# Splitting three down slabs of each hosted feed-forward block, with its convolution taps dealt out anew

## Chip, cores and metric

The kernel runs on one core of a Trainium2 chip. The metric is the device time of one execution in microseconds. TensorE (PE) multiplies, VectorE (DVE), ScalarE (ACT) and GpSimd (POOL) compute elementwise, SyncE (SP) issues the loads.

## The reference

256 tokens and 256 context tokens of width 1024, all in fp32. Three kinds of layers follow one another: a hybrid mixer, a conformer convolution and a window attention, with four feed-forward blocks between them. Two parts matter here.

```python
def conv_ffn(h, w_up, w_dw, b_dw, w_down):          # width 2816, 3 taps
    u = dwconv(h @ w_up, w_dw, b_dw)
    a, b = jnp.split(u, 2, axis=-1)
    return (jax.nn.silu(a) * b) @ w_down
...
    v = a * jax.nn.sigmoid(g)                        # conformer, width 1024
    v = dwconv(v, w_dw, b_dw)                        # 31 taps
    v = jax.nn.silu(layernorm(v, ln_g, ln_b))
    return v @ w_pw2 + b_pw2
```

The first block's feed-forward (ffn0) doesn't depend on the convolution of the context, and that of the context (ffn_ctx) not on the convolution of the tokens, so each can run beside the other.

## The kernel before

Features lie on partitions, tokens along the free axis. All weights come as slabs of 1 MB (`raw`, 128 x 2048 fp32) in a ring of 3 slots, in one fixed order (`KEYS`). Most slabs are split: ScalarE writes the upper part `whi` (fp32r, `hi`), VectorE and GpSimd subtract it for the lower part `wlo` (`lo`, 1536 and 512 columns here), and TensorE makes three fp32r products, upper by upper, upper by lower, lower by upper (`mm3`). A slab in `kept_whole()` isn't split and is multiplied in plain fp32.

A feed-forward block walks 11 pairs j (`NJ`) of 256 hidden columns. Pair j has two up slabs (numbers 3j-1 and 3j) and one down slab (3j+4). TensorE's order is up(j), then down(j-1). An up product is 48 matmuls of 128x256 into bank 2*par or 2*par+1, par = j % 2. In ffn0 and ffn_ctx all down slabs are whole (`DOWN_WHOLE`), 16 fp32 matmuls each, two records apiece in the trace. In ffn_lat and ffn2 they are split, and the middle value too (`m_hi` by ScalarE, `m_lo` by VectorE).

Per pair ScalarE makes `whi` of the next pair's first up slab, the centre tap of half 0 (`tap`), `whi` of the second, the tap of half 1, and silu. VectorE makes its part of `wlo` and the other two taps of a half (`taps`, 4 operations that read PSUM) twice, and then the middle value cvb = silu(a) * b, which the down product reads.

Both blocks also host a 31-tap convolution: v is in `vpad` (in tile `gates`), the sum in `acc` (tile `sra`). Tap 0 with the bias is `dwconv_first`, 8 operations ahead of the block. 22 taps are products by ScalarE (`product`, 8 operations into bufA or bufB in turn) which VectorE adds (`add_product`, one 128x2048 operation); 8 are VectorE's own (`own_tap`, 8 multiply-adds on SBUF). `host(j, par, at)` is called at three places of a pair. Products 3 a pair for j = 2 to 7; an own tap in each of the pairs 0 to 7, after the second add. ScalarE's product n may start when product n-2 has been added. From pair 8 on the layer norm takes the places.

The engines run in order; semaphores bind them. SyncE's load into a slot waits, where the slab before it in the slot is whole, until TensorE has used it (`slab_done`); where it is split, until both lower parts are made (`lo_done`, `lo2_done`). The queue is in order, so the loads behind wait too.

## Time and profile before

| | us |
|---|---|
| median of 3 runs (1394.03 to 1399.96) | 1394.24 |
| the profiled execution, its own time | 1395.78 |
| its span | 1394.0 |
| TensorE busy | 1368.9 (98%) |
| VectorE busy | 963.2 (69%) |
| ScalarE busy | 824.4 (59%) |
| GpSimd busy | 464.9 (33%) |

The span runs from the first instruction to the last; the chain that ended last follows from the last instruction back to what released each. Busy shares are means over stages with different limits, so the two hosted blocks have to be looked at by themselves. Records of matmuls overlap, so one is longer than the step from one to the next; in the timelines of the other engines too neighbours overlap by about 0.08.

### The profile page before, as it was taken

What the parts mean: (1) busy time and instruction counts of PE and PEld (TensorE: products, weight loads), DVE (VectorE), ACT (ScalarE), POOL (GpSimd) and SP (SyncE); (2) the same over time, 40 slices, a digit from 0 to 9 for tenths busy, and PEclk for the clock granted to TensorE, in tenths of its full rate; (3) what the DMA queues carried; (4) which work ended last, traced back from release to release, by engine and by line L of the source; (5) the groups of instructions that cost most, each with busy time, mean ns of one, the idle gap of its engine ahead of it and who ended that gap; (6) DMA issues with size and microseconds to landing.
All of it is one profiled execution on the core that took longest, in us unless ns stands there. A gap on an engine that the chain in (4) does not pass through costs nothing.

```text
span 1394.0 us, 27113 instructions
## 1 busy us (share of the span) xinstructions
PE 1368.9 (98%) x10606; PEld 1270.8 (91%) x10606; DVE 963.2 (69%) x1298; ACT 824.4 (59%) x1190; POOL 464.9 (33%) x190
## 2 busy tenths in 40 slices
PE   7999999999999999999999999999999999999997
PEld 4878889999999999899999999999998868999996
DVE  3312674857899987769899979766667696654446
ACT  3542565645788837567888565555544486644554
POOL 1443434234232321242222201655552201233332
PEclk9999999999999999999999999999999999999999
DMA  8776775455344434774444447556554613455451
GB/s 310 257 272 240 260 281 186 156 218 184 122 181 181 168 153 193 258 279 160 158 160 166 180 189 254 223 213 213 213 185 185 261 47 132 181 181 181 181 184 58
DMA packets 39573, 272.04 MB, mean 195 GB/s; under 512 B 4612, under 2 KB 5892, under 8 KB 6974
## 3 DMA queue, kind: packets, MB, share of 16 engines
q1 hardware_dynamic: 39486, 270.81, 52.1%
q8 instruction: 63, 1.03, 0.3%
q14 instruction: 24, 0.20, 0.0%
HBM read 269.73 MB, written 1.06 MB: 194 GB/s over the span
## 4 chain that ended last, share of the span: by engine, by line
PE 92%; DVE 4%; ACT 2%; DMA 1%; issue 1%; SPq 0%; POOL 0%; DVEq 0%; ACTq 0%
PE ps L1985 23%; PE ps L1986 23%; PE ps L1987 23%; PE ps L655 10%; PE ps L2131 3%; PE ps L2022 2%; DMA raw<-w_dram 1%; PE ps L2032 1%; PE ps L2499 1%; PE ps L2485 1%; DVE wlo L1340 1%; ACT whi L845 1%; PE ps L2434 1%; PE ps L2181 1%; DVE tiny L1833 0%
## 5 line engine op out<-in xcount | busy, mean ns | idle before, releaser
L803 POOL TENSOR_TENSOR wlo<-raw,whi 128x1024 fp32r<-128x1024 f32 (+2 forms) x181 | 462.6, 2557 | 908.9 <-ACT whi L845 908.9
L845 ACT ACTIVATE whi<-raw 128x2048 fp32r<-128x2048 f32 x181 | 345.4, 1911 | 392.6 <-PE ps L1987 232.9
L1340 DVE TENSOR_TENSOR wlo<-raw,whi 128x1024 fp32r<-128x1024 f32 (+2 forms) x181 | 312.7, 1728 | 319.6 <-ACT whi L845 318.7
L1985 PE MATMUL ps<-h_hi,whi 128*128 128x256 f32 x1232 | 354.1, 287 | 0.0
L1986 PE MATMUL ps<-h_lo,whi 128*128 128x256 f32 x1232 | 348.5, 283 | 0.0
L1987 PE MATMUL ps<-h_hi,wlo 128*128 128x256 f32 x1232 | 348.4, 283 | 0.0
L1985 PE MATMUL ps<-g_hi,whi 128*128 128x256 f32 x1040 | 298.4, 287 | 0.0
L1986 PE MATMUL ps<-g_lo,whi 128*128 128x256 f32 x1040 | 294.2, 283 | 0.0
L1987 PE MATMUL ps<-g_hi,wlo 128*128 128x256 f32 x1040 | 294.1, 283 | 0.0
L1985 PEld LDWEIGHTS ps<-h_hi,whi 128*128 128x128 f32 x1232 | 236.0, 192 | 8.1 <-issue 6.8
L1986 PEld LDWEIGHTS ps<-h_lo,whi 128*128 128x128 f32 x1232 | 236.1, 192 | 0.8
L1987 PEld LDWEIGHTS ps<-h_hi,wlo 128*128 128x128 f32 x1232 | 236.1, 192 | 0.0
L1985 PEld LDWEIGHTS ps<-g_hi,whi 128*128 128x128 f32 x1040 | 199.4, 192 | 3.7 <-issue 2.9
L1986 PEld LDWEIGHTS ps<-g_lo,whi 128*128 128x128 f32 x1040 | 199.4, 192 | 0.4
L1987 PEld LDWEIGHTS ps<-g_hi,wlo 128*128 128x128 f32 x1040 | 199.4, 192 | 0.0
L655 PE MATMUL ps<-cvb,raw 128*128 128x256 f32 x704 | 155.3, 379 | 0.0
L655 PEld LDWEIGHTS ps<-cvb,raw 128*128 128x128 f32 x704 | 132.5, 190 | 17.4
L563 DVE SCALAR_TENSOR_TENSOR cvb<-ps,cols,cvb 128x255 f32<-128x255 f32 (+1 forms) x176 | 76.6, 476 | 11.3 <-ACT cvb L485 6.7
L563 DVE SCALAR_TENSOR_TENSOR cva<-ps,cols,cva 128x255 f32<-128x255 f32 (+1 forms) x176 | 76.6, 476 | 10.4 <-ACT cva L485 5.2
L942 ACT ACTIVATE bufB<-gates,cols 128x256 f32 (+1 forms) x176 | 72.7, 499 | 14.6 <-DVE sra L1462 14.6
L942 ACT ACTIVATE bufA<-gates,cols 128x256 f32 (+1 forms) x176 | 72.7, 499 | 13.0 <-DVE sra L1462 13.0
L1985 PE MATMUL ps<-m_hi,whi 128*128 128x256 f32 x208 | 58.9, 283 | 0.0
(317 smaller groups left out, 1858.4 us busy)
## 6 DMA issues: line engine op xcount, KB each, us to landing
raw<-w_dram SPq DMA_DIRECT2D x243, 1024.0 KB, 4.8
sra<-w_dram SPq DMA_DIRECT2D x2, 1024.0 KB, 5.8
mqk<-w_dram SPq DMA_DIRECT2D x2, 1024.0 KB, 6.7
brev<-w_dram SPq DMA_DIRECT2D x2, 1024.0 KB, 7.1
gates<-w_dram SPq DMA_DIRECT2D x2, 1024.0 KB, 8.5
xlat<-xT_dram SPq DMA_DIRECT2D x2, 512.0 KB, 4.6
brev<-w_first_keys_dram SPq DMA_DIRECT2D x1, 1024.0 KB, 9.0
brev<-bias_rows SPq DMA_DIRECT2D x1, 1024.0 KB, 8.5
```

The lines of the kernel that those rows point to most:

```text
L563: ins = dve.scalar_tensor_tensor(out, ps[:, 2 * par + half, m * T + src:m * T + src + n], w, out, ALU.mult, ALU.add)
L655: ins = pe.matmul(ps[:, 4 + m // 2, (m % 2) * T:(m % 2) * T + T], wf[:, k, m * P:m * P + P], cvb[:, par, k, :], start=(first and k == 0 an ...
L803: pool.tensor_tensor(wlo[:, g.slot, part], raw[:, g.slot, part], whi[:, g.slot, part].bitcast(F32), ALU.subtract).then_inc(lo2_done, 1)
L845: act.activation(whi[:, g.slot, :], raw[:, g.slot, :], ACT.Copy).then_inc(hi_done, 1)
L942: ins = act.activation(buf[:, t * T:t * T + T], vpad[:, t, bass.ds(k, T)], ACT.Copy, scale=w)
L1340: dve.tensor_tensor(wlo[:, g.slot, part], raw[:, g.slot, part], whi[:, g.slot, part].bitcast(F32), ALU.subtract)\
L1985: pe.matmul(out, w[0], x[0], start=start, stop=False, skip_group_check=True)
L1986: pe.matmul(out, w[0], x[1], start=False, stop=False, skip_group_check=True)
L1987: return pe.matmul(out, w[1], x[0], start=False, stop=stop, skip_group_check=True)
L2022: pe.matmul(ps[:, bank, m * T:m * T + T], w[i][:, k, m * P:m * P + P], x[0][:, k, :], start=(k == 0 and m == 0 and i == 0), stop=False, sk ...
L2032: ins = pe.matmul(ps[:, bank, m * T:m * T + T], w[:, k, m * P:m * P + P], x[1][:, k, :], start=False, stop=(k == KT - 1), skip_group_check ...
L2131: ins = pe.matmul(ps[r:r + QUAD, bank, 0:SLABC], cnd[:, c:c + QUAD], w[:, t, :], start=(t < 4 and k == 0), stop=(t >= 4 and k == n - 1), s ...
```

## The change

The down slabs of pairs 2, 4 and 6 of ffn0 and ffn_ctx are split (`DOWN_SPLIT`), with the middle value of these pairs, by new semaphores. The taps are dealt out anew: 25 products instead of 22 (three in each of the pairs 0 to 7 and one in pair 8), own taps only in pairs 1, 3, 5, 7, now between the second and the third product, and own tap 2 in front of the block (`early_tap`). `dwconv_first`, that tap and the first two products are made in pieces among the pw1 slabs. In pairs 0 to 7 silu and the middle value come ahead of the second product and its add. In a split pair ScalarE makes the down slab's `whi` and `m_hi`, and VectorE its `wlo` and `m_lo`, ahead of the third product. The pairs of hosted blocks are written out on ScalarE and VectorE instead of a loop.

```diff
-PRODUCTS = 22
+DOWN_SPLIT = (2, 4, 6)
+ADD_SLOTS = [(j, at) for j in range(NJ - 3) for at in range(3)] + [(NJ - 3, 0)]
+OWN_SLOTS = [j for j in range(1, NJ - 3) if j not in DOWN_SPLIT]
+PRODUCTS = len(ADD_SLOTS)
+OWN_TAPS = [2] + [4 * j for j in OWN_SLOTS]
+PRODUCT_TAPS = [k for k in range(1, CONV_TAPS) if k not in OWN_TAPS]
+assert len(PRODUCT_TAPS) == PRODUCTS
...
-            out.append(use != ffn or (i >= 4 and i % 3 == 1))
+            out.append(use != ffn or (i >= 4 and i % 3 == 1 and (i - 4) // 3 not in DOWN_SPLIT))
...
+                if whole and j - 2 in DOWN_SPLIT:
+                    act.wait_ge(hostmid_lo, host_mid(f, j - 2))
                 tap(1, j, par)
-                if host:
+                hosting = host and j < NJ - 3
+                if host and not hosting:
                     host(j, par, 1)
                 act.wait_ge(conv_out, 2 * j + (f * 2 * NJ + 1))
                 act.activation(cva[:, par, :, :], cva[:, par, :, :], ACT.Silu).then_inc(silu_done, 1)
-                if host:
+                if hosting:
+                    host(j, par, 1)
+                if host and not host_split(j, par):
                     host(j, par, 2)
 
             def split(j, par, first):
-                if whole:
+                if whole and not host_split(j, par):
                     return
                 act.wait_ge(mid_f, j + (f * NJ + 1))
+                if whole:
+                    act.wait_ge(slab_done, down_slab(b0, j - 2) + 1)
+                    act.activation(m_hi[:, par, :, :], cvb[:, par, :, :], ACT.Copy).then_inc(hostmid_hi, 2)
+                    host(j, par, 2)
+                    return
...
             if host:
-                with act.Fori(0, 3) as jj:
-                    for u in range(2):
-                        up(Slab(b0 + 5 + 3 * u, 2, jj), 2 * jj + (2 + u), u, False)
-                for j in (NJ - 3, NJ - 2):
-                    up(Slab(b0 + 3 * j - 1), j, j % 2, False)
+                for j in range(2, NJ - 1):
+                    g = Slab(b0 + 3 * j - 1)
+                    up(g, j, j % 2, False)
+                    hi(g + (2 + RING))
+                    split(j, j % 2, False)
...
                 taps(1, j, par)
-                if beside:
+                hosting = beside and j < NJ - 3
+                if beside and not hosting:
                     beside(1)
                 dve.wait_ge(silu_done, j + (f * NJ + 1))
                 dve.wait_ge(conv_out, 2 * j + (f * 2 * NJ + 2))
                 dve.tensor_tensor(cvb[:, par, :, :], cva[:, par, :, :], cvb[:, par, :, :], ALU.mult).then_inc(mid_f, 1)
-                if beside:
+                if hosting:
+                    beside(1)
+                if beside and not host_split(j, par):
                     beside(2)
                 if down:
                     lo(g + (2 + RING))
+                if whole and host_split(j, par):
+                    dve.wait_ge(hostmid_hi, host_mid(f, j))
+                    dve.tensor_tensor(m_lo[:, par, :, :], cvb[:, par, :, :], m_hi[:, par, :, :].bitcast(F32), ALU.subtract)\
+                       .then_inc(hostmid_lo, 2)
+                    beside(2)
...
             pair(Slab(b0 + 2), 1, 1, True, hosted(1, 1))
-            with dve.Fori(0, 3 if host else 4) as jj:
-                order.enter(jj, 8 + (2 * KT if host else 0))
-                for u in range(2):
-                    j = 2 * jj + (2 + u)
-                    pair(Slab(b0 + 5 + 3 * u, 2, jj), j, u, True, hosted(j, u))
-                order.leave(3 if host else 4)
             if host:
-                for j in (NJ - 3, NJ - 2):
+                for j in range(2, NJ - 1):
                     pair(Slab(b0 + 3 * j - 1), j, j % 2, True, hosted(j, j % 2))
...
-                if whole:
+                plain = whole and not host_split(j, par)
+                if plain:
                     pe.wait_ge(landed[g.slot], g.landings())
                     pe.wait_ge(mid_f, j + (f * NJ + 1))
                     wf = raw[:, g.slot, :].rearrange("p (k n) -> p k n", k=2)
                 else:
                     pe.wait_ge(lo_done, g.split() + 1)
                     pe.wait_ge(lo2_done, g.split() + 1)
-                    pe.wait_ge(mid_lo, j + (fs * NJ + 1))
+                    if whole:
+                        pe.wait_ge(hostmid_lo, host_mid(f, j))
+                    else:
+                        pe.wait_ge(mid_lo, j + (fs * NJ + 1))
...
-            def product(q, n, k, buf):
-
-                if not isinstance(n, int) or n >= 2:
+            def product(q, n, t0=0, t1=KT):
+
+                k, buf = PRODUCT_TAPS[n], (bufA, bufB)[n % 2]
+                if n >= 2:
                     act.wait_ge(prod_used, n + (PRODUCTS * q - 1))
-                for t in range(KT):
...
+                else:
+                    act.wait_ge(v_done, 4 * q + t1 // 2)
+                    act.wait_ge(pads_done, 2)
+                for t in range(t0, t1):
+                    ins = act.activation(buf[:, t * T:t * T + T], vpad[:, t, k:k + T], ACT.Copy, scale=col("dw_w", KT * k + t))
+                if t1 == KT:
+                    ins.then_inc(prod_done, 1)
...
                 def host(j, par, at):
-                    if not isinstance(j, int) or j < 2:
-                        early = isinstance(j, int)
-                        if at == 2 and early:
-                            return
-                        if early and j == 0 and at == 0:
-                            act.wait_ge(v_done, 4 * q + 4)
-                            act.wait_ge(pads_done, 2)
-                        n, k = (2 * j + at, 3 * j + (1 + at)) if early else (3 * j + (at - 2), 4 * j + (at - 1))
-                        product(q, n, k, (bufA, bufB)[at if early else (par + at) % 2])
-                    if isinstance(j, int) and (j, at) == (NJ - 2, 1):
+                    if (j, at) == (0, 0) and q == 0:
+                        product(q, 0, 6, KT)
+                        product(q, 1, 6, KT)
+                    if (j, at) in ADD_SLOTS[1:-1]:
+                        product(q, ADD_SLOTS.index((j, at)) + 1)
...
                 hi(Slab(b1 + 3 + RING))
                 glu(q, 2, b1 + 3)
                 hi(Slab(b1 + 4 + RING))
+                act.wait_ge(xlo_done, KT // 2 * n + KT // 2)
+                product(q, 0, 0, 6)
                 hi(Slab(b1 + 5 + RING))
                 glu(q, 3, b1 + 5)
+                product(q, 1, 0, 6)
...
             c = hi_to(c, "pw1_lat", 7)
+            product(1, 0, 0, 6)
             c = hi_to(c, "ffn_ctx", 0)
             c = hi_to(c, "ffn_ctx", 1)
             group_rows("ada_a")
             glu(1, 3, done("pw1_lat", 7) - 1)
             c = hi_to(c, "ffn_ctx", 2)
+            product(1, 0, 6, KT)
+            product(1, 1)
...
                 fold(n, sq)
                 lo(Slab(b1 + 1 + RING))
                 glu(q, 1)
+                dwconv_first(q, 2, 4)
                 scale(n, x, gains, y)
                 lo(Slab(b1 + 2 + RING))
                 split_lo(i, y, out, shift)
                 lo(Slab(b1 + 3 + RING))
                 glu(q, 2)
+                dwconv_first(q, 4, 6)
                 lo(Slab(b1 + 4 + RING))
+                early_tap(2, 6)
                 lo(Slab(b1 + 5 + RING))
                 glu(q, 3)
-
-            def dwconv_first(q):
-
-                dve.wait_ge(v_done, 4 * q + 4)
+                dwconv_first(q, 6, KT)
+                early_tap(6, KT)
...
+            def own_tap(k, t0=0, t1=KT):
+
+                for t in range(t0, t1):
+                    order.mark(dve.scalar_tensor_tensor(acc[:, t, :], vpad[:, t, k:k + T], col("dw_w", KT * k + t), acc[:, t, :],
+                                                        ALU.mult, ALU.add))
+
+            def early_tap(t0, t1):
+
+                dve.wait_ge(dve_order, order.value())
+                own_tap(OWN_TAPS[0], t0, t1)
...
-                    if isinstance(j, int) and j < 2:
-                        if (j, at) == (1, 0):
-                            add_product(q, 1, bufB)
-                        if at == 1:
-                            add_product(q, 2 * j, bufA)
-                            own_tap(q, 2 * j + 1, 3 * j + 3)
-                    elif not isinstance(j, int):
-                        n = 3 * j + (at - 3)
-                        add_product(q, n, bufs[(par + at + 1) % 2])
-                        if at == 1:
-                            own_tap(q, n + 1, 4 * j + 2)
-                    elif (j, at) == (NJ - 3, 0):
-                        add_product(q, PRODUCTS - 1, bufs[(PRODUCTS - 1) % 2])
+                    if at == 2 and j in OWN_SLOTS:
+                        dve.wait_ge(prod_used, ADD_SLOTS.index((j, 1)) + 1 + PRODUCTS * q)
+                        own_tap(OWN_TAPS[1 + OWN_SLOTS.index(j)])
+                    if (j, at) in ADD_SLOTS:
+                        n = ADD_SLOTS.index((j, at))
+                        add_product(q, n, bufs[n % 2])
                     elif (j, at) == (NJ - 3, 2):
...
                 x = flat(xlat[:, 2 * k:2 * k + 2, :])
                 dve.tensor_tensor(x, ps[:, 4 + k, :], x, ALU.add).then_inc(x_ready, 1)
+                if k == 0:
+                    dwconv_first(0, 0, 2)
+                if k == 1:
+                    early_tap(0, 2)
             pw1_dve(0, BASE["pw1_ctx_b"], 2, 2, xlat, bufB, lambda t: col("norm_ffn", t), bufA, G, None)
 
 
-            dwconv_first(0)
...
             c = lo_to(c, "pw1_lat", 6)
+            dve.wait_ge(xlo_done, KT // 2 * 5)
+            dwconv_first(1, 0, 4)
             glu(1, 2)
+            dwconv_first(1, 4, 6)
             c = lo_to(c, "pw1_lat", 7)
+            early_tap(0, 6)
             c = lo_to(c, "ffn_ctx", 0)
             c = lo_to(c, "ffn_ctx", 1)
             glu(1, 3)
+            dwconv_first(1, 6, KT)
             c = lo_to(c, "ffn_ctx", 2)
+            early_tap(6, KT)
             group_add("ada_a")
             modulated(4, 6, mod2_done, GROUPS.index("ada_a") + 1)
 
 
-            dwconv_first(1)
```

VectorE at the end of a pair, in the loop before (par 0): own tap, middle value, add, next lower half.

```order
L1469 ISA
L1469 SCALAR_TENSOR_TENSOR sra<-gates,cols,sra 128x256
L581 REGISTER_ALU
L583 TENSOR_TENSOR cvb<-cva,cvb 128x512
L1458 REGISTER_ALU
L1462 TENSOR_TENSOR sra<-sra,bufB 128x2048
L1339 REGISTER_ALU
L1340 TENSOR_TENSOR wlo<-raw,whi 128x1536
```

The same place after, in a pair with an own tap (3 of ffn0): the middle value stands ahead of add and own tap.

```order
L609 TENSOR_TENSOR cvb<-cva,cvb 128x512
L1510 TENSOR_TENSOR sra<-sra,bufA 128x2048
L1515 SCALAR_TENSOR_TENSOR sra<-gates,cols,sra 128x256 x8
L1510 TENSOR_TENSOR sra<-sra,bufB 128x2048
L1383 TENSOR_TENSOR wlo<-raw,whi 128x1536
```

And in the split pair 4: no own tap, the third lower half and m_lo ahead of the third add.

```order
L609 TENSOR_TENSOR cvb<-cva,cvb 128x512
L1510 TENSOR_TENSOR sra<-sra,bufB 128x2048
L1383 TENSOR_TENSOR wlo<-raw,whi 128x1536
L618 TENSOR_TENSOR m_lo<-cvb,m_hi 128x512
L1510 TENSOR_TENSOR sra<-sra,bufA 128x2048
L1383 TENSOR_TENSOR wlo<-raw,whi 128x1536
```

The add of the third product moved behind two operations that wait for the down slab. ScalarE at the end of a pair, in the loop before: the last of the second product, silu, the first operation of the third.

```order
L942 ISA
L942 ACTIVATE bufB<-gates,cols 128x256
L505 REGISTER_ALU
L506 ACTIVATE cva<-cva 128x512
L939 REGISTER_ALU
L942 ISA
L942 REGISTER_ALU
L942 ACTIVATE bufA<-gates,cols 128x256
```

ScalarE after, split pair 4 of ffn_ctx: silu is ahead of the second product, the down slab's whi and m_hi ahead of the third.

```order
L524 ACTIVATE cva<-cva 128x512
L982 ACTIVATE bufA<-gates,cols 128x256 x8
L882 ACTIVATE whi<-raw 128x2048
L536 ACTIVATE m_hi<-cvb 128x512
L982 ACTIVATE bufB<-gates,cols 128x256 x8
L882 ACTIVATE whi<-raw 128x2048
```

Silu moved one product forward; whi and m_hi stand where the third product began.

## Rows read from the trace of the kernel before

**Rows 1.** The page: the chain that ended last, share of the span by engine.
```profile
PE 92%; DVE 4%; ACT 2%; DMA 1%; issue 1%; SPq 0%; POOL 0%; DVEq 0%; ACTq 0%
```

**Rows 2.** Sums: ffn0, ffn_ctx; PE, PEld, DVE, ACT, POOL busy (count), clock, DMA share, GB/s.
```profile
339.30:543.20 203.90, 203.90 (x1416) 194.61 (x1416) 178.04 (x229) 151.47 (x274) 57.48 (x22) 1.00 0.41 160
624.60:829.00 204.40, 204.40 (x1419) 194.98 (x1419) 186.17 (x234) 151.55 (x274) 52.78 (x23) 1.00 0.42 165
```

**Rows 3.** The chain in order of time (start, us, what): whole down products.
```profile
380.74 6.91 PE ps L655 x32
399.15 6.91 PE ps L655 x32
...
776.93 7.11 PE ps L655 x32
```

**Rows 4.** Timeline of VectorE (start, us, operation, out<-in, count, idle before), ffn0's loop.
```profile
403.02 1.76 DVE L1340 TENSOR_TENSOR wlo<-raw,whi 128x1536 fp32r<-128x1536 f32 x1
...
406.50 2.28 DVE L1462 TENSOR_TENSOR sra<-sra,bufB 128x2048 f32<-128x2048 f32 x1
409.05 3.26 DVE L1469 SCALAR_TENSOR_TENSOR sra<-gates,cols,sra 128x256 f32<-128x256 f32 x8 [0.27 <-DVE sra L1462]
412.22 0.69 DVE L583 TENSOR_TENSOR cvb<-cva,cvb 128x512 f32<-128x512 f32 x1
412.82 2.29 DVE L1462 TENSOR_TENSOR sra<-sra,bufA 128x2048 f32<-128x2048 f32 x1
```

**Rows 5.** Timeline of VectorE, pair 1 of ffn0, written out in front of the loop.
```profile
361.56 1.78 DVE L563 SCALAR_TENSOR_TENSOR cva<-ps,cols,cva 128x254 f32<-128x254 f32 x4
363.26 2.28 DVE L1462 TENSOR_TENSOR sra<-sra,bufB 128x2048 f32<-128x2048 f32 x1
365.46 2.83 DVE L1340 TENSOR_TENSOR wlo<-raw,whi 128x1536 fp32r<-128x1536 f32 x1
...
369.90 2.28 DVE L1462 TENSOR_TENSOR sra<-sra,bufA 128x2048 f32<-128x2048 f32 x1
372.22 3.26 DVE L1469 SCALAR_TENSOR_TENSOR sra<-gates,cols,sra 128x256 f32<-128x256 f32 x8
```

**Rows 6.** Timeline of VectorE, ffn_ctx's loop.
```profile
684.81 1.75 DVE L1340 TENSOR_TENSOR wlo<-raw,whi 128x1536 fp32r<-128x1536 f32 x1
...
690.47 2.83 DVE L1340 TENSOR_TENSOR wlo<-raw,whi 128x1536 fp32r<-128x1536 f32 x1
...
776.06 0.69 DVE L583 TENSOR_TENSOR cvb<-cva,cvb 128x512 f32<-128x512 f32 x1
```

**Rows 7.** Timeline of GpSimd beside it.
```profile
683.97 3.72 POOL L803 TENSOR_TENSOR wlo<-raw,whi 128x512 fp32r<-128x512 f32 x1 [11.04 <-ACT whi L845]
690.30 1.39 POOL L803 TENSOR_TENSOR wlo<-raw,whi 128x512 fp32r<-128x512 f32 x1 [2.61 <-ACT whi L845]
```

**Rows 8.** Timeline of ScalarE: pair 1 of ffn0, and m_hi in ffn_lat.
```profile
363.02 1.90 ACT L845 ACTIVATE whi<-raw 128x2048 fp32r<-128x2048 f32 x1
364.82 1.01 ACT L485 ACTIVATE cvb<-ps,cols 128x256 f32<-128x256 f32 x2
365.72 3.30 ACT L942 ACTIVATE bufB<-gates,cols 128x256 f32<-128x256 f32 x8
368.92 0.62 ACT L506 ACTIVATE cva<-cva 128x512 f32<-128x512 f32 x1
...
901.01 0.61 ACT L516 ACTIVATE m_hi<-cvb 128x512 fp32r<-128x512 f32 x1
```

**Rows 9.** Timelines of VectorE and GpSimd in ffn_lat, where halves are 1024 wide.
```profile
902.28 2.89 DVE L590 TENSOR_TENSOR m_lo<-cvb,m_hi 128x512 fp32r<-128x512 f32 x1
...
901.18 3.44 POOL L803 TENSOR_TENSOR wlo<-raw,whi 128x1024 fp32r<-128x1024 f32 x1 [2.31 <-ACT whi L845]
```

**Rows 10.** Issues of loads, stretch 424.6 to 424.7: the first of three; last number: us to landing.
```profile
raw<-w_dram SPq DMA_DIRECT2D x1, 1024.0 KB, 4.7
```

**Rows 11.** Timeline of VectorE among the last pw1 slabs in front of ffn0.
```profile
341.33 1.76 DVE L1340 TENSOR_TENSOR wlo<-raw,whi 128x1536 fp32r<-128x1536 f32 x1 [4.00 <-ACT whi L845]
```

34 lines of the change are left out of this document (20 added, 14 removed).

## The prediction

> **What bounds the kernel now.** I read the chain that ended last first: 92% of the span is TensorE [rows 1]. Then the sums of two stretches, the two hosted feed-forward blocks ("ffn0" and "ffn_ctx"): TensorE is busy for all of 203.9 and 204.4 us, at a granted clock of 1.00, VectorE for 178.0 and 186.2, ScalarE for 151.5 in each, GpSimd for 57.5 and 52.8 [rows 2]. So whatever shortens TensorE's work there shortens the program, as long as the engines that feed it keep up, and VectorE is near its own limit. The chain shows the period: one whole down product starts 18.41 us behind the other and takes 6.91, which leaves 11.50 for the two up products of 48 matmuls each, 5.75 for one [rows 3]. In the second block one takes 7.11: there VectorE's product cvb starts at 776.06, takes 0.69, and TensorE begins on it at 776.93 [rows 3, 6]. The middle value came just in time.
>
> **TensorE's side.** A split down product has the same 48 matmuls of 128x256 as an up product, so I price it at 5.75 instead of 6.91: 1.16 less. Three slabs in two blocks are 6 x 1.16 = 6.9 us, the most that the change can save. It needs both halves of the slab and of the middle value before TensorE gets there.
>
> **VectorE's work.** Steps from start to start. In the loop: half of a slab 1.68 (1.76 less the 0.08 by which neighbours overlap), own tap 3.17 (409.05 to 412.22), product of the middle value 0.60 (412.22 to 412.82), an added product 2.55 from 406.50 to 409.05 [rows 4]. Written out, as pair 1 is and as all pairs will be: taps 1.70, add 2.20, add with an own tap behind it 2.32 [rows 5]. A pair with an own tap after the change: 2 x 1.68 + 2 x 1.70 + 3 x 2.20 + 0.1 for each side of the own tap + 3.17 + 0.60 = 17.3. A pair with a split slab has no own tap but a third half and m_lo, 0.6 (a 512-wide operation, as the product): 3 x 1.68 + 3.4 + 6.6 + 0.6 + 0.6 = 16.2, and 1.2 if it stands still for GpSimd before m_lo (below). Two pairs: 34.7 for VectorE against 17.25 + 18.41 = 35.7 for TensorE. Before it was 36.8 for TensorE and, in the second block, from 684.81 to 776.06 + 0.6 = 91.9 us for not quite five pairs, with no idle worth the name. So the sum of the work fits, with 1 us in two pairs to spare; the order decides.
>
> **ScalarE's work**: a product 3.20 (365.72 to 368.92), an upper half 1.80, a tap 0.90, silu and m_hi 0.53 each, m_hi's 0.61 less the overlap [rows 8]. A split pair is 3 x 3.2 + 3 x 1.8 + 1.8 + 1.1 = 17.9 us, the other 15.5: 33.4 in two pairs, which fits.
>
> **What is moved in front.** Tap 0 and the first own tap (16 operations, about 6 us) and two products go among the pw1 slabs. VectorE stands idle 4.0 us before one lower half there [rows 11], and each slab is wanted a slab or two later; I price this at nothing. If that cover is gone, the first halves of the block come later by the last piece, tap 0 and own tap of two tiles, 1.6 us. Three more adds and four fewer own taps in a block are in the sums above. The product of the middle value goes ahead of an add and an own tap, 5.4 us earlier; that ends the 0.2 us of the second block, and it is no limit afterwards. SyncE's queue: the load behind a split slab waits for its lower halves and no longer for TensorE, so it goes out earlier; nobody waits for it longer.
>
> **The tight place** is a split slab. Its load can start only when TensorE has ended the down product before (time D). It lands 4.7 after issue [rows 10], D + 4.9; ScalarE's upper half takes 1.9, VectorE's lower half 1.68, GpSimd's part then 1.2 (one ended at 683.97 + 3.72 = 687.7, 1.2 behind VectorE's half [rows 6, 7]), m_lo 0.6: D + 10.4. TensorE wants it after two up products, D + 11.5. Margin 1.1 us, if VectorE is already waiting. Queued behind that wait on VectorE are m_lo, the third add, and the next pair's lower half; on ScalarE behind the landing m_hi, the third product and the next upper half.
>
> **Who waits for whom at a slab's halves.** GpSimd's and VectorE's subtractions never overlap. Where the upper half came while VectorE was in its add, two things are seen: GpSimd began at 690.30 and ended in 1.39 us, and VectorE's half took 2.83 instead of 1.75, 1.1 more; or GpSimd began at 683.97, took 3.72, and VectorE's half, due 0.84 later, took 1.75 [rows 6, 7]. The first is an add that follows the taps, which read ps; the second an add that follows the middle product, another operation on SBUF alone. In ffn_lat m_lo right behind a lower half took 2.89 and ended behind GpSimd's 3.44 [rows 9]. So I take: GpSimd gets in after the first such operation of VectorE in a row, and not later in the row.
>
> The Trainium skill, page SBUF — State Buffer, section "SBUF: two separate sides", says that VectorE and GpSimd share a port pair under an exclusive lock, and that the one that starts first keeps it for its whole instruction while the other blocks. The row at 690.30 agrees; the one at 683.97 doesn't show first come, first served, since GpSimd had waited 0.84 us and VectorE went on. Read as first come, first served, it makes the slower rival below.
>
> **The walk of a split pair.** Start the clock at the second add of the pair before. VectorE: own tap 2.3, add 5.6, lower half 7.8 (own tap and add before it, so not stopped), taps 9.5, add 11.2 to 13.4. ScalarE, released by the same add: product 2.3, upper half 5.5, tap 7.3, product 8.2, upper half 11.4, ready at 13.3. A tie within 0.1 us. D is 13.3 too: VectorE last stood waiting at the split slab before, 6.9 behind that D; from there m_lo 3.5 later, add, half, taps, add, half (0.3 late by ScalarE), taps, product bring the second add to 22.4, and 35.7 - 22.4 = 13.3. Without a stop VectorE ends its add at 19.6, waits for the upper half at 20.1, m_lo ends at 23.6, wanted at 24.8: in time. With a stop of 1.1 at the tie the add ends at 20.7, behind the 20.1; GpSimd then has to wait out half, m_lo and add, 20.7 + 4.5 = 25.2, and ends at 26.4: 1.6 late.
>
> **Forecast.** In the first block VectorE's halves were not stopped in the loop (1.76 at 403.02), in the second one of two was, in each pair [rows 4, 6]. I take the same phases after the change: ffn0 saves 3.45; ffn_ctx saves 3.45 and gives back 2 x 1.6 at slabs 4 and 6 (slab 2 follows the looser pair 1). 6.9 - 3.2 = 3.7 us less. The profiled span is 1394.0, its own time 1395.78, the median of the runs 1394.24; the difference is put on the median: 1394.24 - 3.7 = **1390.5**.
>
> **The rivals.**
> Full saving: the tie falls well in both blocks. For it: ScalarE is released by VectorE's add in both, so that the phase may be the same. Against: nothing keeps the tie. 1394.24 - 6.9 = 1387.3.
> No effect: the tie falls badly in both, 6.9 - 6.4 = 0.5 saved, 1393.7. The split then doesn't do what it says: TensorE works less and waits as much.
> Slower: GpSimd goes first at every half that it waits for. Then VectorE has 34.7 + 5 x 1.1 - 1.1 (the stop before m_lo is in already) = 39.1 us in two pairs against 35.7, and the waits for landed slabs can't give that back. The halves of slab 4 and 6 are then ready at about D + 13.7, 2.2 late each, and the up slabs behind them 0.3 to 1 late, some 2 us more in a block: 6.5 - 3.45 = 3 us slower a block, 1394.24 + 6.1 = 1400.3. It decides from the point where more than one half in two pairs is stopped. For it: the half behind taps and add was stopped in the second block, and m_lo in ffn_lat; against: none of the halves behind product and add was stopped in the second block.
>
> **Chances.** Forecast 35%, full saving 25%, no effect 15%, slower 15%, the rest 10% for what the walk doesn't hold (the own tap itself stopped by GpSimd, a late landing). The unknown with the widest bounds is m_lo, between 0.6 and 2.89 [rows 9], where I take 1.8 with its stop, since GpSimd's part is half as wide here: at 0.6 nothing changes, at 2.89 the margin is just gone and VectorE has 35.8 us in two pairs, level with TensorE, for 0 to 2 us in all. The range reaches from full saving nearly to slower: 1387 to 1399. The forecast's own is 1389 to 1392. About 0.5%, 7 us, is what a measurement can tell from no change; faster by more than that needs all of the 6.9 and something on top: 0.1; slower by more than that needs the slower rival at its upper end: 0.1; the same 0.8.
>
> **What would show it.** Down products of slabs 2, 4, 6 in 5.75, pairs 17.25 and 18.41 apart in the chain. A gap of TensorE in front of the down product of slab 4 or 6, and none at the up products. VectorE idle about 0.5 in front of the lower half of a split slab (full saving), or that half in 1.75 and GpSimd's over 4 us (forecast, second block). The lower half of the second up slab in 1.75 or 2.83 tells who won the tie. Wrong it would be if TensorE waits in pw1 or at its up products in ffn0, if the own tap takes more than 3.3, or if the load of a split slab lands later than 5 us after its issue.

## The result, and the profile after

| | before | after |
|---|---|---|
| median, same chip, 7 runs each, us | 1399.44 | 1408.85 |
| lowest to highest, us | 1394.03 to 1401.88 | 1403.72 to 1412.10 |
| span of the profiled execution, us | 1394.0 | 1409.4 |
| ffn0, first up product to the work behind its last down product, us | 203.71 | 208.51 |
| ffn_ctx, the same, us | 204.34 | 209.79 |
| VectorE busy | 963.2 (69%) | 999.4 (71%) |

The ratio is 1.0085, with a 95% interval from 1.0067 to 1.0104: the changed kernel is slower by 0.85%, some 12 us, and outside the range of the prediction. (The two medians of the table lie 9.4 us apart, with a scatter of 8 us in each column.) The two profiled spans differ by 15.4 us. The two blocks account for 4.8 and 5.45 of it, and 4.5 lie ahead of ffn0, behind waits of TensorE near 70 and 200 us (last section). The pieces moved in front don't make them: with the same program ahead of the block, ffn0 begins at 343.6 us in after and at 337.1 and 337.7 in e6 and e8, against 339.1 in before. So the blocks are what has to be explained: 10.25 us.

The sums of the two blocks after (columns as in [rows 2]), cut at their own bounds:

```profile
343.64:552.15 208.51, 203.12 (x1465) 195.22 (x1463) 193.80 (x204) 165.04 (x297) 49.92 (x24) 0.99 0.42 157
633.72:843.51 209.79, 204.25 (x1468) 195.63 (x1467) 195.97 (x207) 165.16 (x297) 52.27 (x25) 0.99 0.43 161
```

TensorE, busy throughout before, now stands idle for some 5.5 us in each block. VectorE is busy for 194 and 196 of 209 us, 16 and 10 more than before. The page's chain by engine, the line that answers to [rows 1], has VectorE in it with 22% instead of 4%:

```profile
PE 69%; DVE 22%; ACT 4%; issue 2%; DMA 2%; SPq 0%; POOL 0%; DVEq 0%; ACTq 0%
```

What TensorE waited for from 343.6 to 843.6 (us in total, times, longest) is m_lo of the split pairs above all:

```profile
PE ps L2038 <- DVE m_lo L618: 8.7, 5, 2.1
PE ps L2038 <- DVE wlo L1383: 1.7, 3, 0.7
```

The timeline of VectorE in ffn0, pairs 3 to 5, the place of [rows 4]:

```profile
422.22 2.29 DVE L1510 TENSOR_TENSOR sra<-sra,bufB 128x2048 f32<-128x2048 f32 x1
424.43 2.83 DVE L1383 TENSOR_TENSOR wlo<-raw,whi 128x1536 fp32r<-128x1536 f32 x1
427.18 1.77 DVE L588 SCALAR_TENSOR_TENSOR cva<-ps,cols,cva 128x254 f32<-128x254 f32 x4
428.86 2.28 DVE L1510 TENSOR_TENSOR sra<-sra,bufA 128x2048 f32<-128x2048 f32 x1
431.06 2.85 DVE L1383 TENSOR_TENSOR wlo<-raw,whi 128x1536 fp32r<-128x1536 f32 x1
...
438.52 2.85 DVE L1383 TENSOR_TENSOR wlo<-raw,whi 128x1536 fp32r<-128x1536 f32 x1
441.30 0.68 DVE L618 TENSOR_TENSOR m_lo<-cvb,m_hi 128x512 fp32r<-128x512 f32 x1
441.90 2.28 DVE L1510 TENSOR_TENSOR sra<-sra,bufA 128x2048 f32<-128x2048 f32 x1
444.10 2.84 DVE L1383 TENSOR_TENSOR wlo<-raw,whi 128x1536 fp32r<-128x1536 f32 x1
...
450.75 2.86 DVE L1383 TENSOR_TENSOR wlo<-raw,whi 128x1536 fp32r<-128x1536 f32 x1
```

and of GpSimd beside it:

```profile
424.11 1.53 POOL L840 TENSOR_TENSOR wlo<-raw,whi 128x512 fp32r<-128x512 f32 x1 [11.53 <-ACT whi L882]
430.02 2.28 POOL L840 TENSOR_TENSOR wlo<-raw,whi 128x512 fp32r<-128x512 f32 x1 [4.38 <-ACT whi L882]
```

Every half in these rows takes 2.83 to 2.86 us; in the loop of ffn0 before it was 1.76 [rows 4]. GpSimd's instruction begins during VectorE's add (424.11, 430.02) and ends 1.1 to 1.2 us behind it: it takes its turn between the add and the half, and the half waits. From 385 us on this holds for all 16 halves of ffn0 up to the layer norm, and from 677 on for all 16 of ffn_ctx. A timed half is 1.07 us longer; five of them in two pairs make 5.35. From the half at 424.43 to the same one two pairs later, at 463.83, VectorE needs 39.40 us, and TensorE's work is 35.7.

### The profile page after: what moved, and what is told of

Its sections match the earlier page's. It is cut to its first block, busy times and chain, and to the rows that moved or that the text cites. A ratio compares the mean times of both kernels' runs of the same rounds, so it can differ in the third digit from the quotient of the medians.

```text
span 1409.4 us, 26388 instructions
## 1 busy us (share of the span) xinstructions
PE 1370.9 (97%) x10702; PEld 1274.4 (90%) x10702; DVE 999.4 (71%) x1268; ACT 856.9 (61%) x1250; POOL 457.2 (32%) x196
## 4 chain that ended last, share of the span: by engine, by line
PE 69%; DVE 22%; ACT 4%; issue 2%; DMA 2%; SPq 0%; POOL 0%; DVEq 0%; ACTq 0%
PE ps L2038 19%; PE ps L2039 18%; PE ps L2040 18%; DVE wlo L1383 7%; DVE sra L1510 7%; PE ps L2184 3%; PE ps L692 2%; DVE cvb L588 2%; PE ps L2075 2%; DMA raw<-w_dram 2%; DVE sra L1515 1%; DVE cva L588 1%; ACT whi L882 1%; PE ps L2552 1%; PE ps L2085 1%
## 5 line engine op out<-in xcount | busy, mean ns | idle before, releaser
L840 POOL TENSOR_TENSOR wlo<-raw,whi 128x1024 fp32r<-128x1024 f32 (+2 forms) x187 | 454.9, 2434 | 931.8 <-ACT whi L882 931.8
L882 ACT ACTIVATE whi<-raw 128x2048 fp32r<-128x2048 f32 x187 | 356.8, 1911 | 360.4 <-PE ps L2040 234.1
L1383 DVE TENSOR_TENSOR wlo<-raw,whi 128x1024 fp32r<-128x1024 f32 (+2 forms) x187 | 351.0, 1878 | 309.7 <-ACT whi L882 309.5
L692 PE MATMUL ps<-cvb,raw 128*128 128x256 f32 x512 | 112.8, 379 | 0.0
L692 PEld LDWEIGHTS ps<-cvb,raw 128*128 128x128 f32 x512 | 96.4, 190 | 12.6
L982 ACT ACTIVATE bufA<-gates,cols 128x256 f32<-128x256 f32 x208 | 86.1, 500 | 28.4 <-DVE sra L1510 28.4
L2038 PE MATMUL ps<-m_hi,whi 128*128 128x256 f32 x304 | 87.9, 289 | 8.7 <-DVE m_lo L618 8.7
L2040 PE MATMUL ps<-m_hi,wlo 128*128 128x256 f32 x304 | 87.5, 288 | 0.0
L2039 PE MATMUL ps<-m_lo,whi 128*128 128x256 f32 x304 | 87.3, 287 | 0.0
L982 ACT ACTIVATE bufB<-gates,cols 128x256 f32<-128x256 f32 x192 | 79.4, 501 | 9.2 <-DVE sra L1510 9.2
```

The source lines that it names most:

```text
L692: ins = pe.matmul(ps[:, 4 + m // 2, (m % 2) * T:(m % 2) * T + T], wf[:, k, m * P:m * P + P], cvb[:, par, k, :], start=(first and k == 0 an ...
L840: pool.tensor_tensor(wlo[:, g.slot, part], raw[:, g.slot, part], whi[:, g.slot, part].bitcast(F32), ALU.subtract).then_inc(lo2_done, 1)
L882: act.activation(whi[:, g.slot, :], raw[:, g.slot, :], ACT.Copy).then_inc(hi_done, 1)
L982: ins = act.activation(buf[:, t * T:t * T + T], vpad[:, t, k:k + T], ACT.Copy, scale=col("dw_w", KT * k + t))
L1383: dve.tensor_tensor(wlo[:, g.slot, part], raw[:, g.slot, part], whi[:, g.slot, part].bitcast(F32), ALU.subtract)\
L2038: pe.matmul(out, w[0], x[0], start=start, stop=False, skip_group_check=True)
```

## The experiments

"Block" is always the stretch of the table above, read from the one traced execution of each run. It is the sharper measure: where nothing in ffn0 waits and its down slabs are whole it comes out as 203.71 in all six traces (before, e3, e4, e5, e7, e9), while whole runs of one kernel scatter over 4 to 13 us. Ratios are to before on the same chip: its median was 1395.88 beside e1 to e4, 1396.70 beside e5 to e8 and 1395.82 beside e9 to e11.

| run | median, us | ratio to before (95%) | ffn0 | ffn_ctx |
|---|---|---|---|---|
| after | 1408.85 | 1.0085 (1.0067 to 1.0104) | 208.50 | 209.79 |
| e1_pool_behind | 1391.80 | 0.9964 (0.9948 to 0.9980) | 200.31 | 200.81 |
| e2_pool64 | 1393.75 | 0.9982 (0.9963 to 1.0000) | 202.60 | 203.57 |
| e3_nosplit | 1397.21 | 1.0004 (0.9985 to 1.0023) | 203.71 | 204.63 |
| e4_mid_sooner | 1404.25 | 1.0053 (1.0033 to 1.0073) | 203.71 | 210.61 |
| e5_before_behind | 1397.37 | 1.0005 (0.9987 to 1.0023) | 203.71 | 204.20 |
| e6_behind_from_2 | 1388.43 | 0.9952 (0.9936 to 0.9968) | 200.31 | 200.74 |
| e7_head_start | 1401.54 | 1.0022 (1.0000 to 1.0043) | 203.71 | 207.69 |
| e8_old_order | 1395.60 | 0.9996 (0.9976 to 1.0015) | 201.89 | 204.19 |
| e9_slow_product | 1398.03, one run | | 203.71 | 204.13 |
| e10_short_product | 1407.37, one run | | 207.93 | 210.06 |
| e11_sooner_slow_product | 1397.10 | 0.9997 (0.9978 to 1.0017) | 204.64 | 204.69 |

**e1, GpSimd kept out of the way.** The theory is that the port between VectorE and GpSimd, not the added work, makes VectorE late. The edit changes what GpSimd waits for, so that its part falls beside VectorE's taps, which read PSUM.

```diff
-                    pool.wait_ge(hi_done, g.split() + 1)
+                    if KEYS[g.c][0].removesuffix("_end") in DOWN_WHOLE:
+                        pool.wait_ge(lo_done, g.split() + 1)
+                    else:
+                        pool.wait_ge(hi_done, g.split() + 1)
```

> After, but in the two hosted blocks GpSimd's part of a slab waits until VectorE's part is done (lo_done) instead of for the upper half, so it can't take the port between an add and a half of VectorE. Port theory (VectorE is over its budget because GpSimd goes ahead of it at every half, 1.07 us each): halves in 1.75 instead of 2.75, two pairs of VectorE 39.4 - 5 x 1.07 + 1.1 (m_lo stopped instead) = 35.2, under TensorE's 35.7, so both blocks are bound by TensorE again: 203.7 - 3.45 = 200.3 us each instead of 208.5 and 209.8, about 1387 to 1388 beside a before of 1394. Work theory (the third half, m_lo and the third add come too late whatever GpSimd does, since the split slab is landed only 4.9 us behind TensorE's release): TensorE still waits 2 us and more in front of each split down product, blocks of 204 us or more.

Measured: 200.31 and 200.81 us, ratio 0.9964. Work neither added nor removed, and 17 us less than after. The sums:

```profile
337.40:537.70 200.30, 200.30 (x1464) 193.63 (x1463) 179.96 (x204) 164.76 (x297) 33.19 (x24) 1.00 0.44 164
620.70:821.50 200.80, 200.80 (x1467) 194.11 (x1467) 180.12 (x206) 163.65 (x295) 34.32 (x25) 1.00 0.44 168
```

TensorE waits for nothing in either. VectorE in split pair 2 of ffn0:

```profile
388.49 2.28 DVE L1513 TENSOR_TENSOR sra<-sra,bufB 128x2048 f32<-128x2048 f32 x1
392.70 1.76 DVE L1386 TENSOR_TENSOR wlo<-raw,whi 128x1536 fp32r<-128x1536 f32 x1 [1.92 <-ACT whi L885]
394.37 0.69 DVE L618 TENSOR_TENSOR m_lo<-cvb,m_hi 128x512 fp32r<-128x512 f32 x1
394.97 3.39 DVE L1513 TENSOR_TENSOR sra<-sra,bufA 128x2048 f32<-128x2048 f32 x1
398.29 1.75 DVE L1386 TENSOR_TENSOR wlo<-raw,whi 128x1536 fp32r<-128x1536 f32 x1
```

The one turn that GpSimd still takes from VectorE, behind a split slab, now costs the add (3.39 instead of 2.28), after m_lo is done, and nobody waits for it. VectorE is back to waiting for the upper half (1.92). The work theory is out: the split slab is in time, and the split gives all it could. One thing was new, a wait of TensorE ahead of ffn_ctx (e6).

**e2, more work for VectorE.** GpSimd's part of a slab in the hosted blocks is cut from 512 columns to 64.

```diff
-    return 512 if use.removesuffix("_end") in DOWN_WHOLE else 1024
+    return 64 if use.removesuffix("_end") in DOWN_WHOLE else 1024
```

> After, but in the hosted blocks GpSimd gets 64 columns of a slab instead of 512 and VectorE 1984 instead of 1536: VectorE has 0.5 us more work at each of five halves in two pairs. Port theory: halves in 2.2 (2.5 if stopped for the 0.3 of the short part) instead of 2.75, two pairs of VectorE in 36.7 to 38.2 instead of 39.4, so FASTER than after though VectorE has more to do: blocks of 203 to 206 us instead of 208.5 and 209.8. Work theory: VectorE has more work, so two pairs take 39.4 or more and the blocks 209 or more.

Measured: halves of 2.34 where stopped and 2.22 where not, blocks of 202.60 and 203.57: 6 us less each than after, with 29% more columns in every half of VectorE (1984 for 1536). So the 512 columns cost VectorE more when GpSimd has them (1.07 us of standing still) than when it does them itself (2.22 - 1.75 = 0.47).

**e3, the split left out.** All down slabs whole, taps and order as after.

```diff
-DOWN_SPLIT = (2, 4, 6)
+DOWN_SPLIT = ()
...
-OWN_SLOTS = [j for j in range(1, NJ - 3) if j not in DOWN_SPLIT]
+OWN_SLOTS = [1, 3, 5, 7]
...
-            return j in DOWN_SPLIT if isinstance(j, int) else par == 0
+            return False
...
```

> After with all down slabs whole (as in before), the taps dealt out and the middle value made sooner as in after. It tells the split from the rest of the change. VectorE has 39.4 - 2.75 - 0.6 = 36.0 us in two pairs with every half stopped, TensorE 36.8: no wait, both theories expect blocks of 203.7 to 204 us, the time of before within 2 us. If the new order or the pieces in front cost something by themselves, it is slower than before by that. Port theory in addition: VectorE comes to wait for ScalarE's upper half again, goes first, and its halves take 1.75.

Measured: 203.71 and 204.63, no wait of TensorE but 0.2 us in the layer norm; of four halves two were stopped (2.83, 2.85) and two not (1.76), in both blocks. Without the third half and m_lo VectorE gets back to waiting for ScalarE, 2.8 us and then 0.25 us in two pairs, and the two halves behind these waits are the unstopped ones. So taps, pieces in front and order cost nothing by themselves here, since VectorE has the room; it is the split's work that takes this room away.

**e4, only the middle value sooner.** Before, with silu and the middle value ahead of the second product and its add.

The edit on VectorE; ScalarE has the same one:

```diff
+                hosting = beside and (not isinstance(j, int) or j < NJ - 3)
-                if beside:
+                if beside and not hosting:
                     beside(1)
...
                 dve.tensor_tensor(cvb[:, par, :, :], cva[:, par, :, :], cvb[:, par, :, :], ALU.mult).then_inc(mid_f, 1)
+                if hosting:
+                    beside(1)
```

> Before, with one part of the change alone: silu and the middle value ahead of the second product and its add in pairs 0 to 7; own taps in every pair and all slabs whole as before. VectorE's work in two pairs is 34.8 us with no half stopped and 39.1 with all four stopped, against TensorE's 36.8. If the order of the middle value is what lets GpSimd in (in before a half behind own tap, middle value, add wasn't stopped), ffn_ctx and perhaps ffn0 become 2.3 us longer in two pairs, up to 8 us a block. If what counts is that VectorE runs behind ScalarE for lack of time (as after, with its third half), nothing changes: blocks of 203.7 and 204.3 less 0.2 us each for the middle value that comes in time.

Measured: ratio 1.0053. ffn0 keeps 203.71 with the halves of its loop in 1.76, ffn_ctx takes 210.61 with all 12 halves from 671 to 787 us in 2.83 to 2.86, in one program:

```profile
338.60:542.40 203.80, 203.80 (x1417) 194.66 (x1415) 180.01 (x228) 151.14 (x273) 56.41 (x21) 1.00 0.42 160
623.90:834.50 210.60, 206.15 (x1420) 194.89 (x1418) 193.15 (x234) 151.44 (x273) 42.43 (x22) 1.00 0.43 160
```

This is an edit that adds no work and makes a value 5 us sooner, and it costs 6 us in ffn_ctx. In before one half of two was stopped there [rows 6]; now each of these is. Two questions follow: why ffn0 escapes (e7, e11), and why the old order spared one half (e8 to e10).

**e5, the control for e1.** The edit of e1 made to before.

> Before, with the one edit of the run in which GpSimd waits for VectorE's part: in the hosted blocks GpSimd's part waits for VectorE's part instead of for the upper half. Control: how much of that run's time is the edit's own and how much the split's. VectorE has no stopped half then, 34.8 us of work in two pairs against TensorE's 36.8, so both blocks are TensorE's alone: 203.7 (as ffn0 before) and 203.7 instead of 204.34. About 0.6 us less than before in all, perhaps with 1.4 us more in front of ffn_ctx, where GpSimd's first part waits behind two halves of VectorE. The split with the taps is then worth 6.9 us on top, which only comes out when GpSimd keeps out of the way.

Measured: 203.71 and 204.20, all halves in 1.75, ratio 1.0005 (0.9987 to 1.0023). GpSimd's wait by itself gains nothing in before, because TensorE is the bound there either way (what ffn_ctx gains it loses ahead of it, where the stretch between the blocks is 82.96 us instead of 81.57). The gain of e1 is the split's: 203.71 - 200.31 = 3.40 and 204.20 - 200.81 = 3.39.

**e6, a version that beats both.** As e1, from the third slab of a block on (the edit is shown against e1).

```diff
-                    if KEYS[g.c][0].removesuffix("_end") in DOWN_WHOLE:
+                    use, i = KEYS[g.c]
+                    if use.removesuffix("_end") in DOWN_WHOLE and i >= 2:
```

> After, with GpSimd's part waiting for VectorE's part only from the third slab of each hosted block on. In the run with the edit on all slabs TensorE waited 1.5 us in front of ffn_ctx's first up product, which it didn't do after or before: VectorE does the halves of slabs 0 and 1 back to back there, and GpSimd's part of slab 0 had to wait for both. Expected: that wait goes (stretch between the blocks 81.6 us instead of 83.0), blocks stay at 200.3 and 200.8; 1.4 us less than that run, about 8 us less than before: ratio 0.995 to 0.996. If the wait had another cause, the same as that run.

Measured: 1388.43 against 1396.70 of before, ratio 0.9952 (0.9936 to 0.9968). The stretch between the blocks is 81.56 us again (82.97 in e1), blocks of 200.31 and 200.74.

**e7, a head start.** e4's kernel, in ffn_ctx with GpSimd behind VectorE for slabs 2 to 9 alone.

```diff
-                    pool.wait_ge(hi_done, g.split() + 1)
+                    use, i = KEYS[g.c]
+                    if use == "ffn_ctx" and 2 <= i <= 9:
+                        pool.wait_ge(lo_done, g.split() + 1)
+                    else:
+                        pool.wait_ge(hi_done, g.split() + 1)
...
-                while k0 < k1 and not steady(c + k0, c + k1):
+                while k0 < k1 and (use == "ffn_ctx" and k0 < 11 or not steady(c + k0, c + k1)):
```

> Before with silu and middle value made sooner (the run in which ffn0 took 203.7 us with all halves in 1.76, and ffn_ctx 210.6 with all of them in 2.83), and in ffn_ctx alone GpSimd's part of slabs 2 to 9 behind VectorE's; from slab 11 on the loop is as before. If it is the phase that decides (whoever is late stays late: VectorE ahead of ScalarE waits for the upper half, starts first and isn't stopped; VectorE behind is stopped each time and has 39.1 us of work in TensorE's 36.8, so it stays behind), the head start keeps VectorE ahead to the end: halves in 1.76, ffn_ctx 203.7 to 204.3. If something else in ffn_ctx makes GpSimd come first (its operands, ScalarE's timing), the halves from slab 11 on take 2.83 again and the block is 207 or more.

Measured: ffn_ctx 207.69. As long as GpSimd was kept back the halves took 1.76; from the first one let go, at 708.68, they took 2.85, 2.84 and so on. My theory that the phase decides, so that a head start would last, fell: it was lost at once. The rows of e4 show what decides instead. ScalarE's next upper half and VectorE's next lower half hang on the same add, the second of a pair. In ffn_ctx ScalarE (start, us; product, upper half) runs through:

```profile
699.31 3.31 ACT L948 ACTIVATE bufB<-gates,cols 128x256 f32 x8 [4.32 <-DVE sra L1468]
702.52 1.89 ACT L851 ACTIVATE whi<-raw 128x2048 fp32r<-128x2048 f32 x1
```

and VectorE, with own tap and add, is 0.5 us longer on its way; GpSimd starts in that gap:

```profile
699.36 3.25 DVE L1475 SCALAR_TENSOR_TENSOR sra<-gates,cols,sra 128x256 f32<-128x256 f32 x8 [0.27 <-DVE sra L1468]
702.73 2.29 DVE L1468 TENSOR_TENSOR sra<-sra,bufA 128x2048 f32<-128x2048 f32 x1
704.94 2.83 DVE L1346 TENSOR_TENSOR wlo<-raw,whi 128x1536 fp32r<-128x1536 f32 x1
...
704.49 1.66 POOL L809 TENSOR_TENSOR wlo<-raw,whi 128x512 fp32r<-128x512 f32 x1 [11.83 <-ACT whi L851]
```

In ffn0 the same upper half has to wait for its slab, and this puts it behind VectorE:

```profile
394.80 1.92 ACT L851 ACTIVATE whi<-raw 128x2048 fp32r<-128x2048 f32 x1 [0.63 <-DMA raw<-w_dram]
```

So this is a race with a margin of half a microsecond, which a slab's landing turns. That calls for a test from both sides: e10 and e11.

**e8, the old order with the split.** After, with silu and middle value behind the second product again and the own tap behind the second add.

```diff
-                hosting = beside and j < NJ - 3
+                hosting = False
...
-                hosting = host and j < NJ - 3
+                hosting = False
...
-                    if at == 2 and j in OWN_SLOTS:
-                        dve.wait_ge(prod_used, ADD_SLOTS.index((j, 1)) + 1 + PRODUCTS * q)
-                        own_tap(OWN_TAPS[1 + OWN_SLOTS.index(j)])
...
+                        if at == 1 and j in OWN_SLOTS:
+                            dve.wait_ge(prod_used, ADD_SLOTS.index((j, 1)) + 1 + PRODUCTS * q)
+                            own_tap(OWN_TAPS[1 + OWN_SLOTS.index(j)])
```

> After (split and all), but silu and the middle value back behind the second product and its add, and the own tap directly behind the second add, as in before: VectorE's order in the pairs without a split slab is add, own tap, middle value, add, half. In before a half behind that row wasn't stopped in ffn_ctx, though GpSimd had asked 0.9 us earlier. If that comes from the order, one half of five in two pairs is let alone: VectorE 39.4 - 1.1 = 38.3 us, blocks some 4 us shorter than after (204 to 206) unless the later middle value costs it. If it came from the phase of that block, all halves are stopped here too, the blocks take 208 or more, and a later middle value adds to TensorE's wait in front of split down products.

Measured: 201.89 and 204.19, ratio 0.9996: 6 us a block less than after. All 8 halves behind "own tap, middle value, add" took 1.75, though GpSimd had begun 0.87 us before the add ended. VectorE, then GpSimd:

```profile
410.16 3.26 DVE L1515 SCALAR_TENSOR_TENSOR sra<-gates,cols,sra 128x256 f32<-128x256 f32 x8
413.33 0.68 DVE L609 TENSOR_TENSOR cvb<-cva,cvb 128x512 f32<-128x512 f32 x1
413.93 2.28 DVE L1510 TENSOR_TENSOR sra<-sra,bufB 128x2048 f32<-128x2048 f32 x1
416.13 1.75 DVE L1383 TENSOR_TENSOR wlo<-raw,whi 128x1536 fp32r<-128x1536 f32 x1
...
415.35 3.68 POOL L840 TENSOR_TENSOR wlo<-raw,whi 128x512 fp32r<-128x512 f32 x1 [7.96 <-ACT whi L882]
```

GpSimd gets through only when VectorE turns to its taps: its 3.68 us end at 419.03, 1.15 behind the half. More halves went free than the one in five that I expected (VectorE caught up and went first at others). Two halves behind "taps, add, middle value" were stopped, at 428.95 and 677.38, and one m_lo, at 394.71, took 1.79 instead of 0.68.

**e9 and e10, order or lead.** Two readings were left: the row of operations, or how long before the end of the add GpSimd asks (0.87 to 0.92 us in every case behind own tap, middle value and add, all unstopped; 0.39 to 0.54 in every stopped one behind own tap and add). e9 is before with a slower product, which shortens the lead:

```diff
-                    ins = act.activation(buf[:, t * T:t * T + T], vpad[:, t, bass.ds(k, T)], ACT.Copy, scale=w)
+                    for x, n_x in ([(0, T)] if t < 4 else [(0, T // 2), (T // 2, T // 2)]):
+                        ins = act.activation(buf[:, t * T + x:t * T + x + n_x], vpad[:, t, bass.ds(k + x, n_x)], ACT.Copy, scale=w)
```

> Before, with the last four of a product's eight operations on ScalarE cut into two of 128 columns each (12 operations, same result), so a product takes some 0.5 us longer (estimated from 8 operations in 3.20). In ffn_ctx before, 6 of 6 halves behind own tap, middle value, add went unstopped though GpSimd had asked 0.91 us before VectorE's add ended. Now it asks about 0.4 us before. If the order of VectorE's operations lets it keep the port, these halves stay at 1.76 and ffn_ctx at 204.3. If the lead decides (about 0.9 us goes by, 0.2 to 0.5 is stopped, as all halves behind own tap, add were), they take 2.83 as the other halves, and ffn_ctx becomes 208 to 211.

e10 is e4's kernel with a shorter one, which lengthens it:

```diff
-                for t in range(KT):
+                for t in range(KT - 1):
```

> The kernel with the middle value made sooner (own tap, add, half; 2.83 each in ffn_ctx, GpSimd asking 0.5 to 0.6 us before the add ends), with each product of the loop and around it left at seven of its eight operations: one feature tile of each product is left out, so the output isn't the reference's. ScalarE is then 0.4 us sooner and GpSimd asks about 0.95 us before the add ends. If the lead decides, the halves behind own tap, add take 1.76 as in before, with the other halves still stopped, and ffn_ctx is 204 to 206. If the order decides, all stay at 2.83 and ffn_ctx at 210.6.

Measured: in e9 GpSimd asked 0.16 us before the add's end, and 9 of 9 halves behind "own tap, middle value, add" took 1.75; ffn_ctx 204.13. In e10 it asked 0.83 to 0.85 before in ffn0 and 0.92 to 0.94 in ffn_ctx, the lead of before, and 12 of 12 behind "own tap, add" took 2.82 to 2.85. One row of each, VectorE's half and GpSimd's part:

```profile
703.89 1.75 DVE L1341 TENSOR_TENSOR wlo<-raw,whi 128x1536 fp32r<-128x1536 f32 x1
...
703.80 2.97 POOL L803 TENSOR_TENSOR wlo<-raw,whi 128x512 fp32r<-128x512 f32 x1 [9.01 <-ACT whi L845]
```

```profile
709.99 2.83 DVE L1346 TENSOR_TENSOR wlo<-raw,whi 128x1536 fp32r<-128x1536 f32 x1
...
709.14 2.06 POOL L809 TENSOR_TENSOR wlo<-raw,whi 128x512 fp32r<-128x512 f32 x1 [11.43 <-ACT whi L851]
```

The order decides between these two rows, the lead doesn't. e9 and e10 are one execution each, but the cases repeat within it. And e10 had one more result: with less work for ScalarE, ffn0 went from 203.71 to 207.93, since ScalarE now wins the race there too.

**e11, the race from the other side.** e4's kernel with e9's edit.

> The kernel with the middle value made sooner, with the longer products (12 operations instead of 8, some 0.5 us more each): more work for ScalarE. Race theory: behind the second add ScalarE needs 5.1 us (product and upper half) and VectorE 5.6 (own tap and add), so in ffn_ctx GpSimd asks 0.5 before VectorE's half and stops it; with 0.5 more ScalarE comes level or last and VectorE's half of the first up slab takes 1.76 again. Two pairs of VectorE: 39.1 - 2 x 1.07 = 37.0 at most, against TensorE's 36.8: ffn_ctx 204 to 206 instead of 210.6, so the kernel is FASTER by about 5 us with more work on ScalarE. Work theory: ScalarE's longer products delay everything, 210.6 or more.

Measured: 204.64 and 204.69, ratio 0.9997, where e4 had 203.71, 210.61 and 1.0053. ScalarE has 15 us more to do in each block, comes 0.17 us behind VectorE's add instead of 0.5 ahead of its end, and no half is stopped in either block. TensorE has one short wait left in each, for GpSimd's part of a slab (0.7 and 0.3 us). VectorE's add and half in ffn_ctx:

```profile
702.69 2.29 DVE L1469 TENSOR_TENSOR sra<-sra,bufA 128x2048 f32<-128x2048 f32 x1
705.16 1.76 DVE L1347 TENSOR_TENSOR wlo<-raw,whi 128x1536 fp32r<-128x1536 f32 x1 [0.17 <-ACT whi L851]
```

## Why the prediction was wrong

**TensorE's side** was right. e6's blocks are 203.71 - 200.31 = 3.40 and 204.34 - 200.74 = 3.60 us shorter, 7.0 against the 6.9 of six slabs by 1.16.

**VectorE's work** was right but for half a microsecond: with the five turns of GpSimd taken off, two pairs are 39.40 - 5 x 1.07 = 34.05 us, where my sum without a stop was 34.7 - 1.2 = 33.5. m_lo took the 0.6 that stood in the sum (441.30 to 441.90), not 1.8 and not 2.89. My 1.2 for GpSimd stood at the wrong operation: it got in before the half, not before m_lo.

**ScalarE's work** fits, as said. Busy were 165.0 us of a block.

**What is moved in front** costs nothing, as priced: the stage ahead of ffn0 takes TensorE 69.96 us before and after (269.16 to 339.12, 273.68 to 343.64), and between the blocks 81.57 in both.

**The rule for a slab's halves is the step that failed.** I took from rows 4 to 6 that GpSimd gets in after VectorE's first SBUF-only operation in a row and not later. The change put the middle value ahead of the second add, so the row in front of a pair's first half became add, own tap, add, half, and by my rule GpSimd had no place there. It got in 8 times of 8 in after, and 39 of 39 in after, e3, e4, e7 and e10 together (leaving out one in e7 where it asked 0.01 us before the add's end). Where the middle value stands between own tap and add it was kept out, 23 times of 23, in before, e8 and e9. It was also kept out the few times that it asked ahead of a half directly behind an own tap (2 of 2, in e11) or behind "own tap, middle value" (3 of 3, in before and e9), and once behind m_lo and add, where it asked 0.10 us before the end (e8, 398.63). So the kinds of rows that keep it out are more than one, and these few cases don't tell what they have in common. Own tap and half in e11, VectorE and then GpSimd, which asked 0.39 before the own tap's end:

```profile
358.09 3.26 DVE L1476 SCALAR_TENSOR_TENSOR sra<-gates,cols,sra 128x256 f32<-128x256 f32 x8
361.27 1.75 DVE L1347 TENSOR_TENSOR wlo<-raw,whi 128x1536 fp32r<-128x1536 f32 x1
...
360.96 3.20 POOL L809 TENSOR_TENSOR wlo<-raw,whi 128x512 fp32r<-128x512 f32 x1 [10.56 <-ACT whi L851]
```

The six rows of before from which I drew the rule were all "own tap, middle value, add", and the change itself removed that kind. The rule of the Trainium skill that I had set beside it (page SBUF — State Buffer, "SBUF: two separate sides": whoever starts first keeps the port, the other blocks) would have led to the right side here. The traces agree with it in all 32 stopped halves of after and differ in the 23.

**The walk of a split pair** fell with the rule. Its tie at the second up half was no tie: VectorE's add began 1.1 us before GpSimd asked and ended 1.1 behind (428.86, 430.02, 431.06), and GpSimd went first each time.

**The slower rival was the true one**, with its mechanism, its place and its 39.1 us in two pairs (39.40 measured). I gave it 15%, for six rows that spoke against it. I had priced it at 3 us a block, and it measured 4.8 and 5.45: this term was too small. The waits were right: by the starts of its matmuls, less the usual 0.12 between two, TensorE waits for 6.3 and 6.5 us in a block, against the rival's 6.5. Part of it lies at up products (0.5 and 0.8 us, behind 433.32 and 472.46 in ffn0), where the forecast wanted none. What was missing is the clock, which I hadn't in the sum at all. In each block it fell once, behind starts 2.41 and 2.33 us apart (479.12 and 731.68); behind two others, 2.41 and 2.24 apart, at 439.71 and 771.18, it stayed up. Around the split down product of slab 6 in ffn0, the 0.56 in the column of the clock is close to the lower level of 1.2 GHz:

```profile
476.00:481.50 5.50, 3.40 (x29) 3.20 (x28) 5.50 (x4) 3.98 (x10) 3.16 (x1) 1.00 0.26 110
481.50:485.40 3.90, 3.87 (x20) 3.90 (x21) 3.90 (x2) 3.90 (x7) 1.49 (x1) 0.56 0.74 269
485.40:490.00 4.60, 4.60 (x41) 4.60 (x40) 4.57 (x6) 4.60 (x9) 0.87 (x1) 1.00 0.56 173
```

Matmuls stand 0.21 us apart there instead of 0.12, some 18 of them, which is an estimated 1.6 to 1.7 us (18 x 0.09). The sum for ffn0: 203.71 - 3.45 + 6.3 + 1.7 = 208.3, measured 208.5. For ffn_ctx: 204.34 - 3.45 + 6.5 + 1.7 = 209.1, measured 209.8.

**What changed between a close call and a loss** is that VectorE lost its slack. Before, it waited for ScalarE at each half of ffn0's loop and so went first; the third half and m_lo, which the split adds, take that wait away; from then on GpSimd's turn comes in front of every half and keeps VectorE late. e3 shows it without the third half (two of four stopped, no wait of TensorE), e1 with the third half and without GpSimd's turns.

What stays open is why VectorE keeps the port through "own tap, middle value, add, half" and not through "own tap, add, half" or "taps, middle value, add, half" (stopped in 6 of 6 cases in after). The runs show that it is the order and not the lead, nothing more. Nor is it the time since VectorE last read PSUM: "taps, add, own tap, middle value, add" (before) and "taps, middle value, add, own tap, add" (e4, e10) are the same operations, with the half some 8.5 and 8.9 us behind the taps, and only the second kind was stopped.

## What to carry to other kernels

Where VectorE and GpSimd share a job, count VectorE's share of it with GpSimd's turn on top (here 1.07 us for 512 columns that it does itself in 0.47), unless VectorE is sure to start first; and let GpSimd start on VectorE's end, so that its turn falls beside work that reads PSUM. An engine with one microsecond of slack in 36 has that slack only as long as the order of its rivals holds: look for the race that gives it, and price the loss of it as its own case. A pattern read from rows that are all of one kind says nothing of the kind that the change puts in its place.
